# Two instead of four column groups of the output projection inside the last branch's sum

## The chip, the cores and the metric

The kernel runs on one core of a Trainium2 chip, as one program in one launch. The metric is the device time of that program in microseconds (us), the median over several executions. Matrix products run on TensorE (PE; its weight loads are listed as PEld), elementwise work on VectorE (DVE) and ScalarE (ACT), the splitting of weights on GpSimd (POOL), and the transfers of weights are issued by SyncE (SP).

## What is computed

Two layers of an encoder over 512 tokens of width 1024, in float32. The part that matters here is the end of the mixer of each layer:

```python
branches = jnp.stack([o_a, o_b, o_c, o_d], axis=2)
y = jnp.einsum('bsnc,ncd->bsnd', branches, w_branch)
gates = jax.nn.sigmoid(gate_logits.astype(jnp.float32)).astype(xn.dtype).reshape(b, s, N_BRANCH, D_MODEL)
merged = jnp.sum(gates * y, axis=2)
return merged @ w_out
...
x = x + rms_norm(m, ln_post_mix[l])
h = rms_norm(x, ln_pre_ffn[l])
gu = h @ ffn_w_gu[l]
f = (jax.nn.silu(gu[..., :D_FF]) * gu[..., D_FF:]) @ ffn_w_down[l]
x = x + rms_norm(f, ln_post_ffn[l])
```

Each branch output `o` (256 wide) goes through its own projection to 1024 columns, is multiplied by its gates and summed over the four branches; the sum `merged` goes through `w_out` (1024 x 1024).

## The kernel before

**Arithmetic.** Activations lie transposed: 8 column groups (KD) of 128 partitions by 512 tokens. Each float32 operand is kept as two parts of a reduced-precision type, high and low (`h_hi`, `h_lo`; `w_hi`, `w_lo`; `o_hi`, `o_lo`), and a product is three matmuls: high by high, high by low, low by high (`three`, L576; its matmuls are the lines L578, L579 and L580).

**Weights.** They stream from memory in pieces of 128 x 2048 numbers (1 MB) in a fixed order: the four gate pieces of branch C (`gateC0` to `gateC3`), `branchC`, `out0` to `out3` (two column groups of 128 of `w_out` each), then `gu0`, `gu1` and so on for the feed-forward part. Three slots hold them in turn, so a piece takes the slot of the one three places before it: `out1` that of `gateC3`, `out2` that of `branchC`, `out3` that of `out0`, `gu0` that of `out1`. SP waits until PE has finished with the old piece (`wait_freed`, on `main_done`) and issues the transfer (L497). POOL then makes the two parts in four quarters, `w_hi` (L530) and `w_lo` (L534), piece by piece in the stream's order, and reports the whole piece by `piece_split`; PE waits for that count in `wait_piece` (L582). The low part is written over the raw piece.

**The stretch around the change.** Branch C is the last branch. PE makes its eight gated products (`y_bank("C", d)`), six matmuls each. DVE multiplies a product by its gates (L1669), adds the sum of the other branches (L1674), ACT writes the high part of the sum (L1073), DVE the low part (L1360), one column group later in its own order; PE waits for it in `wait_split(l, ("merged", k))` (L930 and L947). Ahead of products 4 to 7 PE waits for sum `d - 4`, and behind each of them stands `project(d - 4)`; `project(4)` to `project(7)` follow. `project(k)` multiplies sum `k` into tiles 0 to 3 of the output projection, so these four tiles, in four PSUM banks (`out_bank`: `work0`, `work1`, `work2`, `pv`), are built together and end together at `k` = 7. At `k` = 0 it waits for piece `out0` ahead of tile 0 and for `out1` ahead of tile 2.

The remaining tiles are made one at a time by `out_tile` (L961), over all eight `k` in one run. Tiles 4 to 7 hold the first half of the tokens (256) for column groups 4 to 7, tiles 8 to 11 the second half. Each waits for its piece: tiles 4, 5, 8 and 9 use `out2`, tiles 6, 7, 10 and 11 `out3`; from tile 6 on it also waits until ACT has evicted earlier tiles. ACT evicts every tile by a square (L1099) and a scaled copy (L1100), and DVE adds the squares (L1405) for the RMS norm. `wait_freed` lets `out3` follow tile 1, `gu0` tile 3:

```python
elif name.startswith("out"):
    sp.wait_ge(main_done, at(l, N_MAIN, WOUT0 + (1, 3, 9, 11)[int(name[3:])] + 2))
```

Of the kernel before, what the change touches and what calls it, by code (L numbers as in the profile page):

```python
# [38 lines left out]
KD = DM // P  # L39
# [32 lines left out]
PIECE = {name: n for n, (name, _) in enumerate(PIECES)}  # L72
# [178 lines left out]
def program(nc, stream, x_in, const_in, params_in, rpb_in, t5_in, hot_in, out):  # L251
# [104 lines left out]
    with ExitStack() as ctx:  # L356
# [212 lines left out]
        def _(pe):  # L569
# [6 lines left out]
            def three(dst, a_hi, a_lo, b_hi, b_lo, first, last, **kw):  # L576

                pe.matmul(dst, a_hi, b_hi, start=first, stop=False, **kw)  # L578
                pe.matmul(dst, a_hi, b_lo, start=False, stop=False, **kw)  # L579
                return pe.matmul(dst, a_lo, b_hi, start=False, stop=last, **kw)  # L580

            def wait_piece(l, n):  # L582
                pe.wait_ge(piece_split, at(l, NP_, n + 1))

            def wait_split(l, name):
                pe.wait_ge(lo_done, at(l, N_SPLIT, SPLIT_AT[name] + 1))
# [236 lines left out]
            for l in range(0, L):  # L823
# [32 lines left out]
                n = PIECE["Dup"]  # L856
# [71 lines left out]
                def project(k):  # L928

                    wait_split(l, ("merged", k))  # L930
                    for m in range(4):
                        n = PIECE[f"out{m // 2}"]
                        if k == 0:
                            wait_piece(l, n)
                        a = 256 * k + P * (m % 2)
                        mm = three(out_bank[m][:, :], w_hi[:, n % SLOTS, a:a + P], w_lo[:, n % SLOTS, a:a + P],
                                   h_hi[:, k, :], h_lo[:, k, :], k == 0, k == KD - 1)
                        if k == KD - 1:
                            mm.then_inc(main_done, 1)

                n = PIECE["branchC"]
                wait_piece(l, n)
                for d in range(KD):
                    if d < 2:
                        wait_main(l, MAIN_AT[("y", "C", d)])
                    elif d >= 4:
                        wait_split(l, ("merged", d - 4))  # L947
                    for k in range(2):
                        if d == 0:
                            wait_split(l, ("o", "C", k))  # L950
                        a = DM * k + P * d
                        mm = three(y_bank("C", d)[:, :], w_hi[:, n % SLOTS, a:a + P], w_lo[:, n % SLOTS, a:a + P],
                                   o_hi[:, k, :], o_lo[:, k, :], k == 0, k == 1)
                    mm.then_inc(main_done, 1)
                    if d >= 4:
                        project(d - 4)
                for k in range(4, KD):
                    project(k)


                def out_tile(m, ks=range(KD)):  # L961

                    d, cols = OUT_TILES[m]
                    n = PIECE[f"out{d // 2}"]
                    if ks[0] == 0:
                        wait_piece(l, n)
                        if m >= 6:

                            pe.wait_ge(kept_done, l * N_KEPT + m - 1)
                    for k in ks:  # L970
                        a = 256 * k + P * (d % 2)
                        mm = three(out_bank[m][:, cols], w_hi[:, n % SLOTS, a:a + P], w_lo[:, n % SLOTS, a:a + P],
                                   h_hi[:, k, cols], h_lo[:, k, cols], k == 0, k == KD - 1)
                    if ks[-1] == KD - 1:
                        mm.then_inc(main_done, 1)

                for m in range(4, KD):
                    out_tile(m)
                out_tile(KD, range(3))
                mean_square(l, "post_mix", 0)  # L980
# [356 lines left out]
        def _(dve):  # L1337
# [175 lines left out]
            def c_scale(l, g0, n):  # L1513

                _, heads = c_heads(g0, n)
                step(l, dve.tensor_tensor(heads, heads, view(r_out, [[n, NT], [1, n], [0, HD]]), ALU.mult))

            def c_gain(l, g0, n, gain):

                _, heads = c_heads(g0, n)  # L1520
                step(l, dve.tensor_tensor(heads, heads, view(param(gain, 0, HD), [[0, NT], [0, n], [1, HD]]), ALU.mult))

            def c_halves(g0, n, f):

                _, heads = c_heads(g0, n)
                w = NT * n * 16
                tmp = [c_sq[:, 1024 * f + w * i:1024 * f + w * i + w].rearrange("p (t g c) -> p t g c", t=NT, g=n) for i in range(4)]
                return heads[:, :, :, 32 * f:32 * f + 16], heads[:, :, :, 32 * f + 16:32 * f + 32], tmp
# [438 lines left out]
```

## Time and profile before

| what | value |
|---|---|
| median of 3 runs | 1818.87 us (1817.61 to 1824.01) |
| the profiled execution | 1817.37 us |
| its span, first to last instruction | 1815.6 us |
| mean granted clock of PE | 0.98 |
| PE busy | 1729.0 us, 95% of the span |
| POOL busy | 1093.5 us, 60% |
| DVE busy | 822.4 us, 45% |
| ACT busy | 445.3 us, 25% |

Busy times are of the profiled execution. An engine's share says how much of the span it worked, and not whether its work lay on the path that sets the end; for that one reads what each engine waited for. Matmuls overlap one another, so the start of one to the start of the next is its pace, and the duration in a row is longer than that.

### The profile page before, as it was taken

The page shows a single profiled execution, that of the slowest core. Times are in us where ns is not written, and L with a number is a line of the kernel's source. Part 1 is how long each engine was busy: PE and PEld are TensorE (multiplying, and loading weights), DVE is VectorE, ACT ScalarE, POOL GpSimd, SP SyncE. Part 2 cuts the span into 40 slices and gives each one's busy share as a digit, 9 for nine tenths or more (in the row PEclk, how much of TensorE's full clock was granted, in tenths as well). Part 3 has the DMA queues.
Part 4 walks back from the last instruction along what each step waited for, and adds up shares of the span by engine and source line. Part 5 has one row for each costly group of instructions (what it writes and reads, how often), then busy time and mean ns, then how long its engine had stood idle before and what let it go on. Part 6 is the DMA issues. An engine that isn't in the chain of part 4 may idle for free. (4 is left out here: it accounts for less than half of the span.)

```text
span 1815.6 us, 22368 instructions
## 1 busy us (share of the span) xinstructions
PE 1729.0 (95%) x8742; PEld 1443.2 (79%) x8742; DVE 822.4 (45%) x1499; ACT 445.3 (25%) x1031; POOL 1093.5 (60%) x1216
## 2 busy tenths in 40 slices
PE   7999999989989999999999999988998999999997
PEld 6788788767788888888987887876776888888886
DVE  6543553763446444310265435467543554443003
ACT  3441413324133111100154323033332411111000
POOL 8536465344368777767685363753534596777674
PEclk9999999899989999999999999999999899999999
DMA  5113222111122322222231131211112123222222
GB/s 202 70 47 110 77 83 80 47 70 47 48 93 79 107 93 93 86 96 96 95 124 70 47 116 49 92 70 47 70 68 71 47 97 110 95 93 79 96 96 79
DMA packets 27465, 151.44 MB, mean 83 GB/s; under 512 B 3611, under 2 KB 6939, under 8 KB 13504
## 3 DMA queue, kind: packets, MB, share of 16 engines
q1 hardware_dynamic: 23600, 141.22, 21.9%
q10 hardware_dynamic: 3760, 8.78, 1.6%
q8 instruction: 70, 1.15, 0.3%
q14 instruction: 35, 0.29, 0.1%
HBM read 147.88 MB, written 4.70 MB: 84 GB/s over the span
## 5 line engine op out<-in xcount | busy, mean ns | idle before, releaser
L530 POOL TENSOR_SCALAR w_hi<-raw 128x512 fp32r<-128x512 f32 (+3 forms) x576 | 364.6, 642 | 680.5 <-DMA raw<-stream 680.4
L534 POOL TENSOR_TENSOR w_lo<-raw,w_hi 128x512 fp32r<-128x512 f32 (+3 forms) x576 | 709.4, 1242 | 0.0
L578 PE MATMUL work<-h_hi,w_hi 128*128 128x512 f32 (+1 forms) x560 | 215.5, 385 | 11.9 <-POOL w_lo L534 8.2
L579 PE MATMUL work<-h_lo,w_hi 128*128 128x512 f32 (+1 forms) x560 | 213.7, 382 | 0.0
L580 PE MATMUL work<-h_hi,w_lo 128*128 128x512 f32 (+1 forms) x560 | 213.6, 381 | 0.0
L687 PE MATMUL main<-h_hi,w_hi 128*128 128x512 f32 x512 | 211.7, 413 | 0.0
L687 PE MATMUL main<-h_lo,w_hi 128*128 128x512 f32 x512 | 210.1, 410 | 0.0
L687 PE MATMUL main<-h_hi,w_lo 128*128 128x512 f32 x512 | 209.0, 408 | 0.0
L578 PE MATMUL main<-h_hi,w_hi 128*128 128x512 f32 (+1 forms) x512 | 181.6, 355 | 10.8 <-POOL w_lo L534 10.8
L579 PE MATMUL main<-h_lo,w_hi 128*128 128x512 f32 (+1 forms) x512 | 180.4, 352 | 0.0
L580 PE MATMUL main<-h_hi,w_lo 128*128 128x512 f32 (+1 forms) x512 | 180.3, 352 | 0.0
L578 PE MATMUL work<-act_hi,w_hi 128*128 128x512 f32 (+1 forms) x396 | 145.1, 367 | 0.0
L580 PE MATMUL work<-act_hi,w_lo 128*128 128x512 f32 (+1 forms) x396 | 144.8, 366 | 0.0
L579 PE MATMUL work<-act_lo,w_hi 128*128 128x512 f32 (+1 forms) x396 | 144.8, 366 | 0.0
L578 PEld LDWEIGHTS work<-h_hi,w_hi 128*128 128x128 f32 x560 | 107.9, 193 | 34.2 <-POOL w_lo L534 9.1
L1358 DVE TENSOR_TENSOR pt_lo<-turn,pt_hi 128x512 fp32r<-128x512 f32 (+2 forms) x128 | 75.5, 591 | 120.9 <-ACT pt_hi L1073 120.2
L580 PEld LDWEIGHTS work<-h_hi,w_lo 128*128 128x128 f32 x560 | 107.8, 193 | 19.5
L579 PEld LDWEIGHTS work<-h_lo,w_hi 128*128 128x128 f32 x560 | 107.9, 193 | 19.2
L578 PEld LDWEIGHTS main<-h_hi,w_hi 128*128 128x128 f32 x512 | 98.6, 193 | 23.6 <-POOL w_lo L534 11.2
L687 PEld LDWEIGHTS main<-h_hi,w_hi 128*128 128x128 f32 x512 | 98.7, 193 | 21.3 <-issue 3.2
L687 PEld LDWEIGHTS main<-h_hi,w_lo 128*128 128x128 f32 x512 | 98.4, 192 | 20.4 <-issue 3.2
L687 PEld LDWEIGHTS main<-h_lo,w_hi 128*128 128x128 f32 x512 | 98.5, 192 | 19.3 <-issue 3.4
(277 smaller groups left out, 3059.1 us busy)
## 6 DMA issues: line engine op xcount, KB each, us to landing
raw<-stream SPq DMA_DIRECT2D x106, 1024.0 KB, 4.8
raw<-stream SPq DMA_DIRECT2D x32, 704.0 KB, 4.0
raw<-stream SPq DMA_DIRECT2D x4, 832.0 KB, 4.7
x<-x_in ACTq DMA_DIRECT2D x4, 512.0 KB, 11.6
t_line<-t_first ACTq DMA_DIRECT2D x2, 1024.0 KB
rpb<-rpb_line ACTq DMA_DIRECT2D x32, 64.0 KB, 3.5
out<-x SPq DMA_DIRECT2D x16, 128.0 KB, 1.7
bias_b<-t_line ACTq DMA_DIRECT2D x2, 768.0 KB, 4.4
```

The lines of the kernel that those rows point to most:

```text
L530: pool.tensor_scalar(w_hi[:, slot, parts[q]], raw[:, slot, parts[q]], 1.0, 0.0, ALU.mult, ALU.add).then_inc(piece_hi, 1)
L534: e = pool.tensor_tensor(w_lo[:, slot, part], raw[:, slot, part], w_hi[:, slot, part].bitcast(F32), ALU.subtract)
L578: pe.matmul(dst, a_hi, b_hi, start=first, stop=False, **kw)
L579: pe.matmul(dst, a_hi, b_lo, start=False, stop=False, **kw)
L580: return pe.matmul(dst, a_lo, b_hi, start=False, stop=last, **kw)
L687: mm = pe.matmul(main[m % 2][:, :], w, (h_lo if which == 1 else h_hi)[:, k, :], start=(s % STEPS == 0), stop=(s % STEPS == STEPS - 1))
L1358: dve.tensor_tensor(dst, src, part.bitcast(F32), ALU.subtract).then_inc(lo_done, 1)
```

## The change

`project(k)` now multiplies sum `k` into tiles 0 and 1 only, which use piece `out0`. Tiles 2 and 3 are made by `out_tile` like the later ones, each over all eight `k` in one run, behind `project(7)` and ahead of tile 4. The banks, the order of the tiles' completion and the code of all other engines stay.

```diff
@@ -928,8 +928,8 @@
                 def project(k):

                     wait_split(l, ("merged", k))
-                    for m in range(4):
-                        n = PIECE[f"out{m // 2}"]
+                    for m in range(2):
+                        n = PIECE["out0"]
                         if k == 0:
                             wait_piece(l, n)
                         a = 256 * k + P * (m % 2)
@@ -974,7 +974,7 @@
                     if ks[-1] == KD - 1:
                         mm.then_inc(main_done, 1)

-                for m in range(4, KD):
+                for m in range(2, KD):
                     out_tile(m)
                 out_tile(KD, range(3))
                 mean_square(l, "post_mix", 0)
```

The order of PE's instructions in layer 0, at `project(0)`. `work0`, `work1`, `work2` and `pv` are the banks of tiles 0 to 3, `main1` is that of product 5; a name's number behind it is its place in memory. Before:

```order
L578 MATMUL work1<-h_hi_50,w_hi_54 128x512 [waits piece_split]
L579 MATMUL work1<-h_lo_51,w_hi_54 128x512
L580 MATMUL work1<-h_hi_50,w_lo_53 128x512
L578 MATMUL work2<-h_hi_50,w_hi_54 128x512 [waits piece_split]
L579 MATMUL work2<-h_lo_51,w_hi_54 128x512
L580 MATMUL work2<-h_hi_50,w_lo_53 128x512
L578 MATMUL pv<-h_hi_50,w_hi_54 128x512 [waits piece_split]
L579 MATMUL pv<-h_lo_51,w_hi_54 128x512
L580 MATMUL pv<-h_hi_50,w_lo_53 128x512
L578 MATMUL main1<-o_hi_57,w_hi_54 128x512 [waits lo_done]
```

The same place in the changed kernel:

```order
L578 MATMUL work1<-h_hi_50,w_hi_54 128x512 [waits piece_split]
L579 MATMUL work1<-h_lo_51,w_hi_54 128x512
L580 MATMUL work1<-h_hi_50,w_lo_53 128x512
L578 MATMUL main1<-o_hi_57,w_hi_54 128x512 [waits lo_done]
L579 MATMUL main1<-o_lo_58,w_hi_54 128x512
L580 MATMUL main1<-o_hi_57,w_lo_53 128x512
```

The six matmuls of tiles 2 and 3, with their wait for `out1`, are gone from between tile 1 and product 5.

The end of `project(7)` in layer 0, on PE, before: the last matmuls of tiles 1, 2 and 3, then tile 4 (`main0`).

```order
L578 MATMUL work1<-h_hi_50,w_hi_54 128x512
L579 MATMUL work1<-h_lo_51,w_hi_54 128x512
L580 MATMUL work1<-h_hi_50,w_lo_53 128x512
L578 MATMUL work2<-h_hi_50,w_hi_54 128x512
L579 MATMUL work2<-h_lo_51,w_hi_54 128x512
L580 MATMUL work2<-h_hi_50,w_lo_53 128x512
L578 MATMUL pv<-h_hi_50,w_hi_54 128x512
L579 MATMUL pv<-h_lo_51,w_hi_54 128x512
L580 MATMUL pv<-h_hi_50,w_lo_53 128x512
L578 MATMUL main0<-h_hi_50,w_hi_54 128x256 [waits piece_split]
```

The same place in the changed kernel, where tile 2 begins with its wait for `out1`:

```order
L578 MATMUL work1<-h_hi_50,w_hi_54 128x512
L579 MATMUL work1<-h_lo_51,w_hi_54 128x512
L580 MATMUL work1<-h_hi_50,w_lo_53 128x512
L578 MATMUL work2<-h_hi_50,w_hi_54 128x512 [waits piece_split]
L579 MATMUL work2<-h_lo_51,w_hi_54 128x512
L580 MATMUL work2<-h_hi_50,w_lo_53 128x512
```

Behind the last matmul of tile 1 there now stand the 24 of tile 2 and the 24 of tile 3, where there were three of each. DVE, ACT, POOL and SP have the same instructions in the same order.

## Rows read from the trace of the kernel before

**Rows 1.** The page, part 1, PE: busy us (share) xinstructions, of every engine

```profile
PE 1729.0 (95%) x8742; PEld 1443.2 (79%) x8742; DVE 822.4 (45%) x1499; ACT 445.3 (25%) x1031; POOL 1093.5 (60%) x1216
```

**Rows 2.** The waits of PE: in total us, times, longest

```profile
PE main L578 <- POOL w_lo L534: 10.8, 2, 5.4
PE work L578 <- POOL w_lo L534: 10.1, 4, 4.1
```

**Rows 3.** Timeline of PE, layer 0: start us, us, instruction [idle before <-releaser]

```profile
468.51 0.39 PE L580 MATMUL work<-h_hi,w_lo 128*128 128x512 f32 x1
473.05 0.79 PE L578 MATMUL work<-h_hi,w_hi 128*128 128x512 f32 x1 [4.14 <-POOL w_lo L534]
...
474.49 0.63 PE L578 MATMUL pv<-h_hi,w_hi 128*128 128x512 f32 x1
474.92 0.63 PE L579 MATMUL pv<-h_lo,w_hi 128*128 128x512 f32 x1
...
476.76 0.40 PE L578 MATMUL main<-o_hi,w_hi 128*128 128x512 f32 x1
...
485.41 0.39 PE L580 MATMUL turn<-o_hi,w_lo 128*128 128x512 f32 x1
...
497.65 0.39 PE L580 MATMUL work<-h_hi,w_lo 128*128 128x512 f32 x1
...
499.24 0.28 PE L578 MATMUL main<-h_hi,w_hi 128*128 128x256 f32 x1
...
504.87 0.28 PE L580 MATMUL main<-h_hi,w_lo 128*128 128x256 f32 x1
510.53 0.58 PE L578 MATMUL main<-h_hi,w_hi 128*128 128x256 f32 x1 [5.38 <-POOL w_lo L534]
...
514.28 0.28 PE L578 MATMUL main<-h_hi,w_hi 128*128 128x256 f32 x1
```

**Rows 4.** Stretches of layer 0: length, busy per engine, clock, DMA, GB/s

```profile
473.00:477.50 4.50, 4.45 (x13) 3.56 (x14) 0.00 (x0) 0.00 (x0) 0.00 (x0) 0.62 0.00 0
477.45:499.24 21.79, 21.79 (x97) 18.02 (x96) 7.22 (x12) 3.64 (x7) 7.38 (x8) 1.00 0.15 51
```

**Rows 5.** Timeline of POOL, layer 0, columns as above

```profile
470.50 2.49 POOL L534 TENSOR_TENSOR w_lo<-raw,w_hi 128x512 fp32r<-128x512 f32 x2
...
490.63 1.20 POOL L530 TENSOR_SCALAR w_hi<-raw 128x512 fp32r<-128x512 f32 x2 [17.64 <-DMA raw<-stream]
...
503.00 1.22 POOL L530 TENSOR_SCALAR w_hi<-raw 128x512 fp32r<-128x512 f32 x2 [4.98 <-DMA raw<-stream]
...
506.02 1.42 POOL L534 TENSOR_TENSOR w_lo<-raw,w_hi 128x512 fp32r<-128x512 f32 x1
...
508.00 2.48 POOL L534 TENSOR_TENSOR w_lo<-raw,w_hi 128x512 fp32r<-128x512 f32 x2
...
582.26 1.64 POOL L530 TENSOR_SCALAR w_hi<-raw 128x512 fp32r<-128x512 f32 x2
...
588.42 3.42 POOL L534 TENSOR_TENSOR w_lo<-raw,w_hi 128x512 fp32r<-128x512 f32 x2
```

**Rows 6.** Timeline of DVE, layer 0

```profile
467.36 0.68 DVE L1669 SCALAR_TENSOR_TENSOR turn<-gates,turn 128x512 f32<-128x512 f32 x1
...
469.29 0.68 DVE L1669 SCALAR_TENSOR_TENSOR main<-gates,main 128x512 f32<-128x512 f32 x1
...
485.84 0.70 DVE L1669 SCALAR_TENSOR_TENSOR turn<-gates,turn 128x512 f32<-128x512 f32 x1 [2.06 <-PE turn L580]
...
487.18 1.45 DVE L1360 SCALAR_TENSOR_TENSOR h_lo<-turn,h_hi 128x512 fp32r<-128x512 f32 x2
...
505.60 0.72 DVE L1405 TENSOR_TENSOR sum_z<-sum_z,sq_z 128x256 f32<-128x256 f32 x1 [2.45 <-ACT sq_z L1099]
```

**Rows 7.** Timeline of PE, layer 1: first matmul after each stall

```profile
1370.01 0.50 PE L578 MATMUL work<-h_hi,w_hi 128*128 128x512 f32 x1 [4.09 <-POOL w_lo L534]
...
1407.54 0.58 PE L578 MATMUL main<-h_hi,w_hi 128*128 128x256 f32 x1 [5.38 <-POOL w_lo L534]
```

## The prediction

> **What bounds the kernel now.** I read the page first: PE is busy 1729.0 of the 1815.6 us of the span, POOL 1093.5, DVE 822.4 [rows 1]. PE sets the time, and what it does not spend on matmuls it spends in waits or at a low clock. So the second view is the waits of PE: two waits of `main` tiles on POOL's `w_lo` hold it for 10.8 us together, 5.4 at the longest, and four waits of `work` tiles for 10.1 us, 4.1 at the longest [rows 2]. The third view, the timeline of PE, puts the four long ones into the stretch that the change rewrites, two per layer, with 4.14 and 5.38 us in layer 0 [rows 3] and 4.09 and 5.38 us in layer 1 [rows 7].
>
> Wait A is inside `project(0)`. PE has done tiles 0 and 1 and wants tile 2, whose weights are in piece `out1`; the split of that piece ends at 470.50 + 2.49 = 472.99 [rows 5], and PE goes on at 473.05 [rows 3]. Wait B is ahead of tile 6, the first that needs `out3`. That piece may only be fetched when `out0` is free, which is after the last matmul of tile 1, started at 497.65 [rows 3]; its split starts at 503.00 and ends at 508.00 + 2.48 = 510.48 [rows 5], and PE goes on at 510.53 [rows 3].
>
> **What each wait costs now.** From 476.76 to 485.41 are 38 matmuls of 512 columns, so a step is 8.65 / 38 = 0.2275 us [rows 3]. Wait A: 473.05 - 468.51 = 4.54 us where a step is 0.23, a loss of 4.31. The clock has fallen by then: 0.62 is granted on average from 473.0 to 477.5, and 1.00 from 477.45 to 499.24 [rows 4]. In the slow part a step is 474.92 - 474.49 = 0.43 us, that is 1.2 GHz instead of 2.4. The nine steps from 473.05 to 476.76 take 3.71 us instead of 2.05: a loss of 1.66. Wait B: tiles 4 and 5 are 48 matmuls of 256 columns from 499.24 to 504.87, 47 steps of 0.120 us; 510.53 - 504.87 = 5.66 loses 5.54. Behind it, 18 steps take 514.28 - 510.53 = 3.75 us instead of 2.16, a loss of 1.59 [rows 3]. One layer loses 4.31 + 1.66 + 5.54 + 1.59 = 13.10 us. Layer 1 shows waits of the same length [rows 7], so I take twice this: 26.2 us, 1.44% of the span.
>
> **The change, part by part.** No matmul is added or taken away: the 48 of tiles 2 and 3 (24 each) move from eight groups of six to two runs of 24 behind `project(7)`. DVE, ACT, POOL and SP keep their instructions and their order. I put the new order on the clock of layer 0, from 468.51, the last matmul that is the same.
>
> 1. Gate product 5 starts at 468.51 + 0.23 = 468.74. Product (6 steps, 1.37 us) and project (now 6 steps, 1.37 us) alternate: product 6 at 471.47, product 7 at 474.20 with its last matmul at 475.34, `project(4)` at 476.93, 5 at 478.29, 6 at 479.66, 7 at 481.02, its last matmul at 482.16. Tile 2 starts at 482.39, far behind 472.99, where `out1` is ready by the same POOL rows, whose cause (the gates' last matmul) the change does not touch. Wait A goes whole. What it is worth: 5.97 us.
> 2. PE now goes through the sums twice as fast, so the next suspect is DVE, which makes them. Unhindered, DVE needs 469.29 - 467.36 = 1.93 us per column group [rows 6]; PE's pace is 2.73 while products run and 1.37 after. The low half of a sum follows the next product: it starts 487.18 - 485.84 = 1.34 us after that product does on DVE and takes 0.7 [rows 6]. So sum 3 is ready at 469.29 + 2.04 = 471.3, and product 7 wants it at 474.20. DVE takes product 5 at 469.29 + 1.93 = 471.22: sum 4 is ready at 473.3, wanted at 476.93. It takes product 6 at 473.15: sum 5 at 475.2, wanted at 478.29. The last matmul of product 7 now starts at 475.34; before, 485.41 led to DVE's start at 485.84 [rows 3, 6], a lag of 0.43, and from there to the end of the last two low halves there were 487.18 + 1.45 - 485.84 = 2.79 us [rows 6]. So sum 6 is ready at 475.77 + 2.04 = 477.8, wanted at 479.66, and sum 7 at 475.77 + 2.79 = 478.6, wanted at 481.02. The smallest margin is 1.8 us: cost nothing. If this cover were gone, PE would fall back to DVE's 1.93 per group.
> 3. `out2` takes the slot of the last branch's weights. The lag from the last matmul of product 7 to the start of the split was 490.63 - 485.41 = 5.22 us [rows 3, 5]; now 475.34 + 5.22 = 480.56, and with 7.48 us for a split (503.00 to 510.48) it ends at 488.0. Tile 4 wants it at 499.24 - 5.97 = 493.27. Nothing.
> 4. `out3` takes the slot of `out0`, free after the last matmul of tile 1. Tile 1 now ends with `project(7)`, at 482.16, since the groups of tiles 2 and 3 no longer stand between its own. The lag was 503.00 - 497.65 = 5.35 [rows 3, 5]: landed at 487.5, taken by POOL when `out2` is done at 488.0, ready at 495.5. Tile 6 wants it at 493.27 + 5.75 = 499.02. Wait B goes too, with 3.5 us to spare: 7.13 us.
> 5. The first piece of the feed-forward part takes the slot of `out1`, free with tile 3. Tile 3 ends just ahead of tile 4 in both orders, so this transfer keeps its place against PE, and it no longer queues behind `out3` on POOL. ACT's evictions of tiles 2 and 3 come apart from those of 0 and 1, with 5.5 us for each where it needs about one. From tile 6 on all engines stand to each other as before, 13.1 us earlier.
>
> One row speaks against step 4. A `w_lo` quarter beside a DVE sum of two SBUF tiles (505.60) took 1.42 us, the two after it 1.24 each [rows 5, 6], and the slowest splits of the feed-forward part take 588.42 + 3.42 - 582.26 = 9.58 us [rows 5]. The change moves the splits of `out2` and `out3` beside such sums. With 9.58 us for both, `out3` is ready at 480.56 + 19.16 = 499.72, 0.7 us late per layer. That is the bound above; the nearest rows are the same pieces in the same place, 7.48, and I take these. The Trainium skill ("SBUF — State Buffer", Who interferes with whom) says that a VectorE instruction with two SBUF inputs and a GpSimd one that reads SBUF exclude each other for a whole instruction. The row of 1.42 agrees in direction; by the rule the two sums that meet the split of `out2` would cost, at 0.72 us as in the row of 505.60, at most 1.4 us, still inside the margin.
>
> **The sum.** The profiled execution took 1817.37 us (span 1815.6, 1.8 around it); less 26.2 it is 1791.2. The median of the three runs is 1.5 us higher, 1818.87, and would give 1792.7. I forecast 1792. A measurement of this kernel can tell about 0.5%, 9.1 us, from no change; the gain is almost three times that.
>
> **The rivals.**
> - *DVE becomes the bound* (chance 0.06). If margins in step 2 are eaten, the last four groups go at 1.93 instead of 1.37 us: 4 x 0.56 x 2 layers = 4.5 us given back, 1796.5. For it: PE's work per sum is halved. Against: every margin is 1.8 us or more.
> - *Only wait A goes* (0.03). If `out3` is not fetched earlier, or the time saved is waited for in front of the feed-forward part, 2 x 5.97 = 11.9 us are left: 1805.4. For it: POOL takes pieces strictly in turn. Against: the slot of `out0` is free 15 us sooner.
> - *The change does nothing* (0.01): PE waits for `out1` at the same place. The order of instructions speaks against it; 1817.
> - *Slower* (0.02): PE's clock falls in the rewritten stretch and stays low. The place is product 5 to tile 3, 66 matmuls in eleven groups, most behind a wait on DVE, and then the 48 of tiles 2 and 3. A step costs 0.43 - 0.23 = 0.20 us more. It decides from 66 slow matmuls per layer, 13.2 us, just what the waits give back; all 114 cost 22.8 us per layer, so 1817.4 - 26.2 + 45.6 = 1836.8. For it: behind both waits the clock was low. Against: in the same alternation, with more banks, it was 1.00 for 21.79 us with PE busy throughout [rows 4]. The Trainium skill ("TensorE: Matmul & The Clock Gate", A second HAM failure mode) describes a kernel whose short idle times between groups, cycling through PSUM banks, made the clock swing; the trace here shows no such idle time.
> - The forecast: 0.88.
>
> **How the numbers follow.** Down from 1792: the low stretches behind the waits that remain may come out shorter; they cost about 1.6 us each where I could count them, so for two or three of them 4 us: 1788. Up: DVE as bound 1796.5, `out3` late by 0.7 us twice, and the low clock of some other stretch up to 2 us longer: 1800. Beyond it lie the last three rivals, 0.06. Faster by over 0.5%: the forecast, the first rival and two thirds of the second, 0.96; within 0.5%: the rest of that and the change that does nothing, 0.02; slower: 0.02.
>
> **What would show it.** Right: no wait on `w_lo` of over 1 us among PE's waits; product 5 a step after `project(0)`; the split of `out3` directly behind that of `out2`; PE busy and the clock at 1.00 from product 5 to tile 8; everything from tile 6 of layer 0 on some 13 us earlier, and 26 from tile 6 of layer 1 on. Wrong: waits of PE on `h_lo` in `project(4)` to `project(7)` (first rival), on `w_lo` at tile 6 (second), a step of 0.43 us with no wait ahead of it (the slower one).

## The result, and the profile after

Four executions each gave a median of 1792.58 us for the changed kernel (1785.92 to 1793.13) against 1820.4 us before: the ratio is 0.9843, 95% interval 0.9818 to 0.9867. The profiled execution took 1793.13 us, with a span of 1791.2 us, against 1817.37 and 1815.6.

The page's first part, the line that answers to [rows 1]:

```profile
PE 1721.5 (96%) x8742; PEld 1437.5 (80%) x8742; DVE 822.3 (46%) x1499; ACT 445.7 (25%) x1031; POOL 1095.5 (61%) x1216
```

PE is busy 7.5 us less in the same 8742 matmuls, which fits fewer of them at the low clock (the mean granted clock is 0.984, before 0.980). The rest of the 24.4 us is waiting: the waits on `w_lo` fell from 20.9 us in all to 2.4, and the others grew by 1.6 us in all. The waits of PE, the same view as [rows 2], and with it the longest that are left:

```profile
PE pv L578 <- DVE pt_lo L1358: 23.6, 8, 4.0
PE work L578 <- DVE h_lo L1360: 9.8, 10, 4.4
PE turn L650 <- ACT sq_z L1099: 3.3, 2, 1.7
PE work L578 <- POOL w_lo L534: 2.4, 2, 1.4
```

No `main` tile waits for `w_lo` any more, and the `work` tiles do so twice, 1.4 us at the longest, both outside the stretch (at 19.08 and at 901.31, the start of each layer). What is left at the top, eight waits of `pv` tiles on `pt_lo` inside the attention heads, was 23.5 us before and is 23.6 now. The timeline of PE in layer 0, columns as in [rows 3]. It begins with the third gated product; this execution reached it 2.41 us later than that of before (465.71 against 463.30), and all rows of this fence stand that much later than on the clock of the prediction:

```profile
465.71 0.39 PE L578 MATMUL turn<-o_hi,w_hi 128*128 128x512 f32 x1
...
469.57 0.39 PE L580 MATMUL main<-o_hi,w_lo 128*128 128x512 f32 x1
...
471.15 0.39 PE L578 MATMUL main<-o_hi,w_hi 128*128 128x512 f32 x1
...
477.73 0.39 PE L580 MATMUL turn<-o_hi,w_lo 128*128 128x512 f32 x1
...
484.53 0.39 PE L580 MATMUL work<-h_hi,w_lo 128*128 128x512 f32 x1
...
495.63 0.28 PE L578 MATMUL main<-h_hi,w_hi 128*128 128x256 f32 x1
...
501.39 0.28 PE L578 MATMUL main<-h_hi,w_hi 128*128 128x256 f32 x1
...
508.23 0.50 PE L647 MATMUL turn<-const,sum_z 128*128 128x1 f32 x4
```

Product 5 starts at 471.15, product 7 ends with the matmul of 477.73, `project(7)` with that of 484.53; tile 2 follows one step later, tile 4 starts at 495.63, tile 6 at 501.39. Less 2.41 these are 468.74, 475.32, 482.12, 493.22 and 498.98; the prediction had 468.74, 475.34, 482.16, 493.27 and 499.02. No row of the stretch shows an idle time. Its windows, columns as in [rows 4]; the three stretches are the products and sums from product 5 on, tiles 2 and 3, and tiles 4 and 5:

```profile
471.15:484.80 13.65, 13.65 (x62) 11.30 (x61) 8.98 (x15) 3.52 (x7) 6.18 (x8) 1.00 0.22 78
484.80:495.63 10.83, 10.83 (x49) 8.97 (x48) 2.72 (x3) 2.89 (x6) 10.83 (x11) 1.00 0.27 97
495.63:501.39 5.76, 5.76 (x50) 5.75 (x49) 2.05 (x2) 1.92 (x4) 4.31 (x6) 1.00 0.49 182
```

PE is busy throughout and the clock is 1.00. POOL's splits of `out2` (from 482.99), `out3` (from 490.96) and the first feed-forward piece (from 500.69), which answer to [rows 5]:

```profile
482.99 1.20 POOL L530 TENSOR_SCALAR w_hi<-raw 128x512 fp32r<-128x512 f32 x2 [7.47 <-DMA raw<-stream]
...
488.46 2.54 POOL L534 TENSOR_TENSOR w_lo<-raw,w_hi 128x512 fp32r<-128x512 f32 x2
490.96 1.64 POOL L530 TENSOR_SCALAR w_hi<-raw 128x512 fp32r<-128x512 f32 x2
...
496.26 2.99 POOL L534 TENSOR_TENSOR w_lo<-raw,w_hi 128x512 fp32r<-128x512 f32 x2
500.69 1.20 POOL L530 TENSOR_SCALAR w_hi<-raw 128x512 fp32r<-128x512 f32 x2 [1.45 <-DMA raw<-stream]
```

`out3` is split right behind `out2`, as forecast. DVE, which answers to [rows 6], at the last sums and at one of the sums of squares:

```profile
478.15 0.70 DVE L1669 SCALAR_TENSOR_TENSOR turn<-gates,turn 128x512 f32<-128x512 f32 x1 [0.60 <-PE turn L580]
...
479.49 1.45 DVE L1360 SCALAR_TENSOR_TENSOR h_lo<-turn,h_hi 128x512 fp32r<-128x512 f32 x2
...
496.46 1.63 DVE L1405 TENSOR_TENSOR sum_z<-sum_z,sq_z 128x512 f32<-128x512 f32 x1 [4.34 <-ACT sq_z L1099]
```

The last two low halves end at 479.49 + 1.45 = 480.94, 478.53 on the prediction's clock, where 475.77 + 2.79 = 478.56 stood.

### The profile page after: what moved, and what is told of

The parts are those of the page before. It is cut to its first block and busy times, and to the rows that moved or that the text cites. A ratio compares the mean times of both kernels' runs of the same rounds, so it can differ in the third digit from the quotient of the medians.

```text
span 1791.2 us, 22368 instructions
## 1 busy us (share of the span) xinstructions
PE 1721.5 (96%) x8742; PEld 1437.5 (80%) x8742; DVE 822.3 (46%) x1499; ACT 445.7 (25%) x1031; POOL 1095.5 (61%) x1216
## 5 line engine op out<-in xcount | busy, mean ns | idle before, releaser
L1358 DVE TENSOR_TENSOR pt_lo<-turn,pt_hi 128x512 fp32r<-128x512 f32 (+2 forms) x128 | 75.5, 591 | 123.3 <-ACT pt_hi L1073 122.6
L687 PEld LDWEIGHTS main<-h_hi,w_hi 128*128 128x128 f32 x512 | 98.5, 192 | 21.4 <-issue 3.2
L687 PEld LDWEIGHTS main<-h_lo,w_hi 128*128 128x128 f32 x512 | 98.5, 192 | 19.2 <-issue 3.4
L579 PEld LDWEIGHTS main<-h_lo,w_hi 128*128 128x128 f32 x512 | 96.9, 189 | 12.6
```

The costliest lines, as they stand in the source:

```text
L687: mm = pe.matmul(main[m % 2][:, :], w, (h_lo if which == 1 else h_hi)[:, k, :], start=(s % STEPS == 0), stop=(s % STEPS == STEPS - 1))
L1358: dve.tensor_tensor(dst, src, part.bitcast(F32), ALU.subtract).then_inc(lo_done, 1)
```

## The experiments

The stretch is best compared by itself: from the third gated product of branch C, the first that goes to a `turn` bank, to the first matmul on the sum of squares of the first half of the tokens (L647). For before this is 463.30 to 518.95, for the changed kernel 465.71 to 508.23. It holds the same matmuls in all versions. The last row of the changed kernel's fence above is its end; before, it was this one of the same view:

```profile
518.95 0.50 PE L647 MATMUL turn<-const,sum_z 128*128 128x1 f32 x4
```

| version | layer 0, us | layer 1, us | both, against before | median, us | ratio to before (95%) |
|---|---|---|---|---|---|
| before | 55.65 | 55.94 | | 1820.4 | |
| changed | 42.52 | 42.51 | -26.56 | 1792.6 | 0.9843 (0.9818 to 0.9867) |
| wait A away alone | 49.41 | 49.76 | -12.42 | 1802.7 | 0.9908 (0.9890 to 0.9926) |
| wait B away alone | 48.26 | 48.54 | -14.79 | 1803.0 | 0.9905 (0.9887 to 0.9923) |
| slot of `out3` late | 51.59 | 51.85 | -8.15 | 1809.5 | 0.9940 (0.9925 to 0.9955) |
| one group with the sums | 44.33 | 44.33 | -22.93 | 1792.8 | 0.9849 (0.9834 to 0.9864) |
| changed, once more | 42.51 | 42.51 | -26.57 | 1791.8 | 0.9849 (0.9832 to 0.9867) |
| second squares late | 42.51 | 42.51 | -26.57 | 1784.1 | 0.9805 (0.9792 to 0.9819) |

Each ratio is to the runs of before of its own series; their median was 1819.8 in the two later ones. The version of the last row changes what comes behind the stretch.

**Wait A away alone.** In the kernel before, tiles 2 and 3 join the sums at `project(2)` and catch up there (the lines that follow take `kk` in place of `k`):

```diff
                     wait_split(l, ("merged", k))
-                    for m in range(4):
+                    parts = [(m, k) for m in range(2)]
+                    if k == 2:
+                        parts += [(m, kk) for kk in range(3) for m in (2, 3)]
+                    elif k > 2:
+                        parts += [(m, k) for m in (2, 3)]
+                    for m, kk in parts:
...
```

> Takes wait A away alone. Tiles 0 and 1 go with every sum as in the changed kernel, tiles 2 and 3 join at project(2), where they catch up on k = 0 and 1, so that out1 (split ready about 473.0 on the clock of layer 0) is no longer waited for, while tile 1 still ends late, with twelve matmuls in every project. My theory (two separate waits, each with its own stretch of low clock): PE no longer waits for w_lo in the sums, the wait of 5.4 us ahead of tile 6 stays in both layers, gain 2 x 5.97 = 11.9 us, about 1808. Rival (only wait A ever mattered, the second follows from it): both waits gone, 1794. Rival (out1 was not what PE waited for): as before, 1820.

Measured: the stretch is 12.42 us shorter, the time 1802.7. Its timeline of PE has no idle time in the sums, and in front of tile 6 the old wait:

```profile
503.20 0.58 PE L578 MATMUL main<-h_hi,w_hi 128*128 128x256 f32 x1 [5.39 <-POOL w_lo L534]
```

So `out1` was what PE waited for in the sums, and the second wait does not follow from the first. The median lies 5 us under the 1808 that I expected, though the stretch gave only 0.5 us more than forecast. The spans of the profiled executions differ by 14.6 us: 12.42 in the stretches, 1.3 ahead of that of layer 0 (reached at 461.98, before at 463.30) and 0.9 elsewhere. The rest of the 5 us is within the spread of the executions (1801.06 to 1807.91, before 1815.86 to 1822.98); the last section tells of one source of such differences.

**Wait B away alone.** The changed kernel, with the wait for `out1` put back where it was:

```diff
                         if k == KD - 1:
                             mm.then_inc(main_done, 1)
+                    if k == 0:
+                        wait_piece(l, PIECE["out1"])
```

> Takes wait B away alone: the changed kernel, but PE still waits for out1 at the end of project(0), though it does not use it yet. My theory: a wait of 4.1 to 4.5 us on w_lo ahead of gate product 5 in both layers with a step of 0.43 us behind it for some nine steps; no wait ahead of tile 6; 1792.6 + 11.9 = 1804.5, that is 14.3 + 1.6 less than before. Rival (the clock does not fall from the wait, but from the many banks): the wait without the slow steps, 1801.

Measured: 14.79 us off the stretch. PE's timeline has wait A, with slow steps behind it, and none ahead of tile 6:

```profile
472.57 0.80 PE L578 MATMUL main<-o_hi,w_hi 128*128 128x512 f32 x1 [4.08 <-POOL w_lo L534]
473.16 0.63 PE L579 MATMUL main<-o_lo,w_hi 128*128 128x512 f32 x1
473.59 0.63 PE L580 MATMUL main<-o_hi,w_lo 128*128 128x512 f32 x1
474.01 0.63 PE L578 MATMUL main<-o_hi,w_hi 128*128 128x512 f32 x1
```

The steps are 0.43 us, in a kernel whose sums go to two banks and not four; the low clock belongs to the wait and not to the banks. Both halves together give 12.42 + 14.79 = 27.2 us, the change itself 26.6: the two waits are separate and their prices add. The 0.6 us too much lies in the slow steps behind the wait that stays, counted from start to start as in the prediction: behind wait B they cost 1.4 and 1.7 us in the two layers with wait A away, where the kernel before paid 1.6 and 1.9; behind wait A 1.5 and 1.7 with wait B away, where it paid 1.7 and 1.7.

**The slot of `out3` late.** The changed kernel, with the transfer let go after tile 3:

```diff
-                    sp.wait_ge(main_done, at(l, N_MAIN, WOUT0 + (1, 3, 9, 11)[int(name[3:])] + 2))
+                    sp.wait_ge(main_done, at(l, N_MAIN, WOUT0 + (3, 3, 9, 11)[int(name[3:])] + 2))
```

> Tests what took wait B away: the changed kernel, but the transfer of out3 is let go after tile 3 and not after tile 1. My theory (the early end of tile 1 is all of it): last matmul of tile 3 at 493.05 on the clock of layer 0, plus 5.35 us to the start of the split and 7.5 for it, is 505.9, wanted at 499.0: a wait of some 6.9 us on w_lo ahead of tile 6 in each layer and 1.6 us of low clock behind it, 17 us in all, 1809.5. Rival (the transfer was early enough anyway, and POOL or the evictions by ACT set tile 6): no more than 2 us of wait, 1793 to 1796.

Measured: 18.4 us longer in the stretch than the changed kernel, where 17 were expected, and 1809.5 us. Rows of POOL and of PE:

```profile
496.41 1.21 POOL L530 TENSOR_SCALAR w_hi<-raw 128x512 fp32r<-128x512 f32 x2 [9.55 <-DMA raw<-stream]
...
501.38 2.48 POOL L534 TENSOR_TENSOR w_lo<-raw,w_hi 128x512 fp32r<-128x512 f32 x2
```

```profile
503.91 0.58 PE L578 MATMUL main<-h_hi,w_hi 128*128 128x256 f32 x1 [6.65 <-POOL w_lo L534]
504.29 0.42 PE L579 MATMUL main<-h_lo,w_hi 128*128 128x256 f32 x1
504.51 0.41 PE L580 MATMUL main<-h_hi,w_lo 128*128 128x256 f32 x1
504.72 0.41 PE L578 MATMUL main<-h_hi,w_hi 128*128 128x256 f32 x1
```

The split ends at 501.38 + 2.48 = 503.86 and PE goes on at 503.91, 6.65 us late. The wait is as long as expected; the slow steps behind it cost 2.3 us in layer 0 and 2.6 in layer 1, and not 1.6: that is where the 1.4 us over the 17 come from. Wait B is made by the moment at which tile 1 lets the slot go; no eviction and nothing on POOL stands in its place when that is mended.

**One group with the sums.** `for m in range(1)` in `project`, and `for m in range(1, KD)` for `out_tile`.

> Tests the cover of step 2 (DVE makes the sums faster than PE uses them): only tile 0 goes with the sums, tiles 1 to 3 follow one by one. PE's pace is then 0.68 us per sum after the last product, DVE's 1.93. My theory: sums 5, 6 and 7 are late by 0.3, 1.2 and 0.1 us more or less, waits of PE on h_lo of 1.5 to 2 us per layer in the sums, no wait ahead of tile 6 (out3 ready at 497.8, wanted at 500.8): 1792.6 + 3.6 = 1796, or 1798 if the clock falls with them. Rival (PE is bound by its matmuls alone here too): 1792.6.

Measured: 1.82 us more per layer in the stretch, 3.63 in all. The timeline of PE at `project(5)` and `project(6)`:

```profile
473.90 0.39 PE L580 MATMUL work<-h_hi,w_lo 128*128 128x512 f32 x1
474.47 0.50 PE L578 MATMUL work<-h_hi,w_hi 128*128 128x512 f32 x1 [0.18 <-DVE h_lo L1360]
474.81 0.40 PE L579 MATMUL work<-h_lo,w_hi 128*128 128x512 f32 x1
475.05 0.40 PE L580 MATMUL work<-h_hi,w_lo 128*128 128x512 f32 x1
476.39 0.51 PE L578 MATMUL work<-h_hi,w_hi 128*128 128x512 f32 x1 [0.95 <-DVE h_lo L1360]
```

An idle time in a row counts from the end of the matmul before, and matmuls overlap. From start to start sum 5 is late by 474.47 - 473.90 - 0.23 = 0.34 us and sum 6 by 476.39 - 475.05 - 0.23 = 1.11, where 0.3 and 1.2 were expected. The step right after each wait is 0.1 us longer too (474.81 - 474.47 = 0.34 instead of 0.23); these are 1.7 of the 1.82 us. Layer 1 has the same two waits. That is DVE's limit, met with one group and not with two. The median, 1792.8 where 1796 was expected, does not show these 3.6 us against 1792.6 and 1791.8: the executions of the changed kernel spread over 7 us, twice as much.

**The changed kernel once more.**

> The changed kernel once more, as the partner of the next run and for the spread between executions. The rewritten stretch itself (third gated product of branch C to the first sum-of-squares matmul) should take 42.5 us in both layers, 13.1 and 13.4 less than before, whatever the total does; the total 1792.6 with some 3 us of spread, from low stretches of PE's clock elsewhere that come and go.

Measured: 42.51 us in both layers, within 0.01 of the first time. Five executions lay between 1788.06 and 1795.21.

**A version meant to beat both.** A wait that the change leaves is the next one on the way: in the first gate-up piece PE has to put the second half's squares between two steps and waits there for DVE and ACT.

```diff
                 for k in range(KD):
                     first_gate_up(0, k)
-                    if k == 1:
+                    if k == 5:
                         mean_square(l, "post_mix", 1)
```

> A version meant to beat both: the changed kernel, with the matmuls on the squares of the second half (mean_square, post_mix, 1) behind the sixth and no longer behind the second step of the first gate-up piece. There PE now waits 0.7 us for DVE's sum and 1.7 us for ACT's square in each layer, and a stretch of low clock follows. Theory: PE does four more steps in that time, is held only by the normalized input as DVE delivers it, and reaches the next piece some 3 to 4 us sooner per layer: 6 to 8 us, 1785 to 1787. Rival (the stretch is bound by DVE's chain and then by POOL's sum of squares for the second half, so the wait only moves): 1792.

Measured: 1784.06 us (1783.05 to 1785.15), ratio to before 0.9805 (0.9792 to 0.9819); the changed kernel beside it on the same chip 1791.77. The place in the timeline of PE, of the changed kernel and of this version:

```profile
522.26 0.58 PE L647 MATMUL turn<-const,sum_z 128*128 128x1 f32 x4 [0.67 <-DVE sum_z L1405]
524.50 1.01 PE L650 MATMUL turn<-const,sq_z 128*128 128x1 f32 x4 [1.67 <-ACT sq_z L1099]
```

```profile
523.46 0.50 PE L647 MATMUL turn<-const,sum_z 128*128 128x1 f32 x4
523.82 0.58 PE L650 MATMUL turn<-const,sq_z 128*128 128x1 f32 x4
```

The two waits are gone. From the third gated product to the first matmul on the next sum of squares (L661) the changed kernel took 82.38 and 82.40 us, this version 77.79 and 78.48: 8.5 us less, where 6 to 8 were expected. Against the changed kernel's execution of this series, 79.76 and 82.55, it is 6.0 us. Some of the gain is clock, as the last section shows. Whether a place other than the sixth step is better still was not tried.

## Why the prediction was right

- *Both waits go* (steps 1 and 4): right, and shown apart. Wait A was put at 2 x 5.97 = 11.9 us and measured 12.42 alone; wait B at 2 x 7.13 = 14.3 and measured 14.79 alone. The stretch became 26.56 us shorter where 26.2 stood. Nearly all of the 0.36 us more came from layer 1, which I had set equal to layer 0: its stretch became 13.43 us shorter, that of layer 0 13.13. The waits of layer 1 were no longer, but the slow steps behind its wait B cost 1.9 us and not 1.6.
- *DVE keeps up* (step 2): right; no wait on `h_lo` in the sums, and the last low half came within 0.1 us of what was worked out. The experiment with one group shows where the cover ends. The first rival falls.
- *The splits* (steps 3 and 4): the place was right, the duration was short. `out2` took 488.46 + 2.54 - 482.99 = 8.01 us and `out3` 496.26 + 2.99 - 490.96 = 8.29, where I had taken 7.48 for each [rows 5]. `out3` was ready at 499.25 and wanted at 501.39, a margin of 2.1 us instead of 3.5. The bound of 9.58 was not reached. The row that I had weighed with the Trainium skill ("SBUF — State Buffer", Who interferes with whom) pointed the right way: these splits, now beside DVE's sums of two SBUF tiles, ran 0.5 and 0.8 us longer than the 7.48. That 7.48 itself held one such sum (the row of 505.60); the split of `out2` before, which met none, took 495.48 + 2.53 - 490.63 = 7.38. Nobody waited for the longer splits. The end of the one that met no sum, of before:

```profile
495.48 2.53 POOL L534 TENSOR_TENSOR w_lo<-raw,w_hi 128x512 fp32r<-128x512 f32 x2
```

- *Feed-forward part* (step 5): right. PE's waits behind tile 6 are those of before to 0.1 us, 0.67 and 1.67 us at the second sum of squares where 0.56 and 1.66 stood, 13.0 us earlier on the prediction's clock. The first feed-forward piece was split from 500.69 on, and PE did not wait for it.
- *The clock stays up* (the slower rival falls): 1.00 through the stretch. That rival's count was wrong: from product 5 to `project(7)` there are three products and seven sums, 60 matmuls in ten groups and not 66 in eleven (the 13.65 us of the window are 60 steps of 0.2275). All of them slow would have cost 12.0 us per layer, a little less than the waits give back, and with tiles 2 and 3 108 matmuls cost 21.6 us and not 22.8, which puts the price of that rival at 1834.4 instead of 1836.8. Neither the sum nor the range uses it.
- *The signs*: one does not hold as it was written, no wait on `w_lo` of over 1 us. At the start of layer 1 PE waits 1.44 us for `w_lo`, before 1.23. That wait lies outside the stretch and was there before the change.
- *The total*: 1792.0 against 1792.6. That it fits to half a microsecond is luck. The profiled execution came to 1793.13 where the sum gave 1791.2. It had gained 26.56 us in the stretch, and the two spans differ by 24.4: 2.41 us had been lost ahead of the stretch, in code that the change does not touch. The last section shows where most of it went.

## What to carry to other kernels

When weights stream through a ring of slots, the order of the tiles does two things: it sets when a piece is first needed and when its slot comes free, and the second can cost more than the first (14.8 against 12.4 us for the two layers here). Building four tiles together needs two pieces early and frees both late; building two together and the others one by one needs one early and frees it early. What limits this is the engine that makes the input: with two tiles per sum DVE was fast enough, with one it was not.

## What the runs showed of the hardware beside this

**The same wait is followed by the low clock in one execution and not in another.** In both kernels PE waits 3.18 us in branch B of layer 0 for the same low half (L1358). PE's timeline at the end of it, and the window of 5 us from 370 on, of before:

```profile
368.63 0.39 PE L578 MATMUL pv<-pt_hi,v_hi 128*128 128x256 f32 x1 [3.18 <-DVE pt_lo L1358]
```

```profile
370.00:375.00 5.00, 5.00 (x27) 4.12 (x26) 2.58 (x4) 1.58 (x3) 0.00 (x0) 1.00 0.01 3
```

The same two of the changed kernel:

```profile
369.39 0.39 PE L578 MATMUL pv<-pt_hi,v_hi 128*128 128x256 f32 x1 [3.18 <-DVE pt_lo L1358]
```

```profile
370.00:375.00 5.00, 5.00 (x21) 4.29 (x20) 2.59 (x4) 1.57 (x3) 0.00 (x0) 0.67 0.01 3
```

In the first PE kept 1.00, with 27 matmuls in 5 us; in the second it had 0.67, and 21. The changed kernel's execution was 0.76 us late when the wait ended and 2.41 us at the third gated product: 1.65 us were lost here. Of seven profiled executions in which this wait was 3.13 to 3.18 us, five (those of the changed kernel first, wait A away, slot late, one group, second squares late) had steps of 0.43 us soon behind it, and two (before, wait B away) had none. The same happened between two executions of the changed kernel itself, behind the waits of 0.64 to 0.67 and 1.66 to 1.67 us at the second sum of squares; windows of 10.5 us from the matmul that follows the waits:

```profile
524.50:535.00 10.50, 10.50 (x66) 10.50 (x67) 4.59 (x19) 2.48 (x7) 7.46 (x9) 0.72 0.00 1
```

```profile
523.40:533.90 10.50, 10.50 (x88) 10.50 (x89) 6.82 (x24) 4.87 (x14) 7.65 (x10) 1.00 0.00 1
```

With 0.72 granted, 66 matmuls fit, with 1.00, 88. Up to the next sum of squares (L661) that made 82.38 against 79.76 us, 2.6 us. So of the gain of the last experiment in layer 0, 4.6 us, only 2.0 is left against an execution whose clock did not fall. In layer 1 the clock fell at this place in both profiled executions of the changed kernel (0.70 granted over the 10.5 us behind the waits, from 1408.19 and from 1406.80) and stayed at 1.00 in the version without them (1405.24 to 1416.00). That the missing waits are the reason fits this, and so does the spread (four executions of that version lie within 2.1 us, five of the changed kernel within 7.2), but no run shows it by itself. All ten waits on `w_lo` of 4.1 to 6.7 us in these versions were followed by slow steps, at a cost of 1.4 to 2.6 us each, the most behind the two longest. Why a shorter one is followed by them only sometimes, these runs don't settle. The Trainium skill ("TensorE: Matmul & The Clock Gate", What's actually happening) says that the counting runs freely and is not tied to the kernel's start, so that the phase differs from one execution to the next; that fits, and no run here tests it.

**POOL and DVE slow each other both ways.** Beside POOL's split of `out3`, DVE's sum of squares of 512 columns took 1.63 us (the row of 496.46 above), where before, with POOL idle, it took 0.69:

```profile
501.22 0.69 DVE L1405 TENSOR_TENSOR sum_z<-sum_z,sq_z 128x512 f32<-128x512 f32 x1 [0.37 <-ACT sq_z L1099]
```

The splits took 8.0 and 8.3 us instead of 7.4 and 7.5. This is read from rows that lie side by side; no run takes the overlap away by itself. Moving a split earlier can put it beside other work and make it longer; here 3.5 us of margin covered that.
